# A hybrid decoder layer: the weight sums for the down projection move from VectorE to GpSimd, and the work around the end of the up projection is put in another order

## The reference

```python
h = h + rms_norm(mix @ w_out, attn_post_g)          # mix: two attention groups of 8 heads
u = rms_norm(h, mlp_pre_g)
a = jnp.square(jax.nn.relu(u @ w_up))               # w_up 1024 x 4096
h = h + rms_norm(a @ w_down, mlp_post_g)            # w_down 4096 x 1024
```

## Time and profile before

| | |
|---|---|
| device time, median of 3 runs | 611.48 us (611.33 to 612.48) |
| the profiled execution's own time | 612.76 us |
| its span, first to last instruction | 611.0 us |
| TensorE busy | 580.5 us (95%) |
| VectorE busy | 410.3 us (67%) |
| ScalarE busy | 310.6 us (51%) |
| GpSimd busy | 108.8 us (18%) |

### The profile page before, as it was taken

The page is one execution under the profiler, slowest core; times in us unless marked ns, Lnnn a source line. Parts: engine busy times, 40 slices in busy tenths (PEclk is TensorE's granted clock), DMA queues, the critical chain, the costliest instruction groups (busy, mean ns, idle before and its releaser), DMA issues.

```text
span 611.0 us, 8355 instructions
## 1 busy us (share of the span) xinstructions
PE 580.5 (95%) x2900; PEld 483.4 (79%) x2900; DVE 410.3 (67%) x787; ACT 310.6 (51%) x651; POOL 108.8 (18%) x165
## 2 busy tenths in 40 slices
PE   7999999999999999999999999999869999999995
PEld 7988898887787788997777777777748888888874
DVE  3448582788788408427657747757857897777797
ACT  5563262788898324544353352354324566555571
POOL 1153200346798101300000000000000000000034
PEclk9999999999999999999999999999998999999998
DMA  8441412000120082055877877777697555554503
GB/s 301 127 131 55 169 70 69 1 1 1 70 70 1 17 294 70 0 207 197 293 267 271 272 280 263 270 291 263 230 348 274 179 193 198 208 195 172 185 1 137
DMA packets 43777, 101.45 MB, mean 166 GB/s; under 512 B 3937, under 2 KB 22113, under 8 KB 39649
## 3 DMA queue, kind: packets, MB, share of 16 engines
q1 hardware_dynamic: 42704, 101.04, 46.9%
q10 hardware_dynamic: 1040, 0.00, 0.1%
HBM read 82.16 MB, written 18.87 MB: 165 GB/s over the span
## 4 chain that ended last, share of the span: by engine, by line
PE 59%; DVE 20%; ACT 10%; issue 5%; DMA 4%; DVEq 1%; SPq 0%; ACTq 0%; POOL 0%; POOLq 0%
PE bank L1188 19%; PE bank L1189 18%; PE bank L1190 18%; ACT w_hi L509 8%; DVE w_lo L797 6%; DVE stage L1083 5%; DVE relu L1062 3%; PE bank L1358 2%; DMA w_raw<-in_w_down 1%; DVE pT_lo L794 1%; ACT probs L621 1%; DVE bank L926 1%; DMA x_sb<-in_x 1%; DMA stage<-in_w_down 1%; DVE w_lo L794 1%
## 5 line engine op out<-in xcount | busy, mean ns | idle before, releaser
L1188 PE MATMUL bank<-uT_hi,w_hi 128*128 128x512 f32 (+1 forms) x280 | 105.5, 377 | 8.1 <-DVE w_lo L797 8.1
L1190 PE MATMUL bank<-uT_hi,w_lo 128*128 128x512 f32 (+1 forms) x280 | 103.9, 371 | 0.0
L1189 PE MATMUL bank<-uT_lo,w_hi 128*128 128x512 f32 (+1 forms) x280 | 103.9, 371 | 0.0
L509 ACT ACTIVATE w_hi<-w_raw 128x1024 fp32r<-128x1024 f32 (+2 forms) x65 | 62.7, 1010 | 72.4 <-PE bank L1190 63.8
L797 DVE SCALAR_TENSOR_TENSOR w_lo<-w_raw,g_up,w_hi 128x256 fp32r<-128x256 f32 x128 | 52.1, 481 | 66.9 <-ACT w_hi L509 66.9
L794 DVE TENSOR_TENSOR w_lo<-w_raw,w_hi 128x1024 fp32r<-128x1024 f32 (+1 forms) x57 | 67.8, 1232 | 40.8 <-ACT w_hi L509 40.6
L1188 PE MATMUL bank<-w_hi,a_hi 128*128 128x512 f32 x224 | 88.6, 396 | 6.9 <-DVE w_lo L794 6.9
L1189 PE MATMUL bank<-w_lo,a_hi 128*128 128x512 f32 x224 | 88.1, 393 | 0.0
L1190 PE MATMUL bank<-w_hi,a_lo 128*128 128x512 f32 x224 | 87.9, 392 | 0.0
L749 ACT ACTIVATE act_sb<-relu 128x512 f32 (+1 forms) x32 | 20.3, 635 | 106.1 <-DVE relu L1062 106.1
L1188 PEld LDWEIGHTS bank<-uT_hi,w_hi 128*128 128x128 f32 x280 | 52.7, 188 | 22.2 <-issue 13.5
(11 more groups left out here) (148 smaller groups left out, 1042.5 us busy)
## 6 DMA issues: line engine op xcount, KB each, us to landing
w_raw<-in_w_up SPq DMA_DIRECT2D x16, 1024.0 KB, 5.3
stage<-in_w_down SPq DMA_DIRECT2D x16, 1024.0 KB, 4.9
pair_sums<-stage SPq DMA_DIRECT2D x16, 1024.0 KB, 4.0
w_raw<-pair_sums SPq DMA_DIRECT2D x16, 1024.0 KB, 4.7
w_raw<-in_w_down SPq DMA_DIRECT2D x12, 1024.0 KB, 5.8
w_raw<-in_w_in SPq DMA_DIRECT2D x6, 1024.0 KB, 5.8
w_raw<-in_w_out SPq DMA_DIRECT2D x4, 1024.0 KB, 4.8
x_sb<-in_x SPq DMA_DIRECT2D x8, 256.0 KB, 6.0
```

The lines of the kernel that those rows point to most:

```text
L509: return nc.scalar.activation(out, whole, ACT.Copy, scale=scale)
L1188: nc.tensor.matmul(out, lh, rh, start=start, stop=False)
L1189: nc.tensor.matmul(out, lh, rl, start=False, stop=False)
L1190: return nc.tensor.matmul(out, ll, rh, start=False, stop=stop)
```

## The change

1. **Block sums on GpSimd.** `block_sums` leaves DVE. GpSimd does the same four differences for pairs 0 to 14, in straight-line code that waits for each load.
2. **The second bank's square.** ACT's square of bank m=1 of a half-step moves behind the high parts of the next chunk (`activation`).
3. **Activation parts of down chunk 0** (`down_a_hi(0)`, `down_a_lo(0)`), made after up step 0 before, are made with those of chunks 1 and 2 ahead of the last up step.
4. **Raw tile of chunk 2.** `raw_more[0]` moves to memory of its own behind `stage[1]`, and the chunk is loaded before chunk 1, with no wait for the end of up.
5. **Last pair.** Pair 15 is no longer staged. Its raw rows are loaded as chunk 23, the last of pass two, and DVE makes its four sums there, two in chunk 21 and two in chunk 22 (`last_block_sums`).
6. **Order near the end.** DVE's combines are spread: four before the low part of chunk 25, two after it, four after that of chunk 26. The squares of the first two row tiles' first halves move to chunk 12 on ACT, and GpSimd's scaling of them with it. The other squares and `scaled_y(2, 0)` come after the last chunk's parts.

```diff
-        raw_more = [sb(f"w_raw{i + 2}", [P, CW]) for i in range(2)]
+        raw_more = [None, sb("w_raw3", [P, CW])]
+        in_place_of_uT = sb("in_place_of_uT", [P, CW])
...
+        raw_more[0] = sb("w_raw2", [P, CW])
...  SP
-            for j in range(2):
-                down_chunk(j)
-                next_sums(NF // 4, j)
-            for j in range(2):
-                sp.wait_ge(stage_sums, 4 * (NF // 2 + j - 1))
-                store_sums(j, NF // 2 + j - 2)
+            down_chunk(0)
+            next_sums(NF // 4, 0)
+            down_chunk(2)
+            down_chunk(1)
+            for j in (1, 0):
+                sp.wait_ge(stage_sums, 4 * (NF // 2 - 1 - j))
+                store_sums(j, NF // 2 - 2 - j)
...  GpSimd
+            for n in range(NF // 2 - 1):
+                b11, b12, b21, b22 = (stage[n % 2][:, TOP * q:TOP * q + TOP] for q in range(4))
+                pool.wait_ge(stage_in[n % 2], 16 * (n // 2 + 1))
+                for m, (total, a, b) in enumerate(((b11, b12, b11), (b12, b22, b12), (b22, b22, b11), (b21, b21, b22))):
+                    if m:
+                        pool.wait_ge(stage_sums, 4 * n + m)
+                    nc.gpsimd.tensor_tensor(total, a, b, ALU.subtract).then_inc(stage_sums, 1)
...  ScalarE
+            def activation(i, tile):
+                act.wait_ge(relu_c, i * 4 + (tile + 1))
+                nc.scalar.activation(act_sb[:, bass.ds(i * 4 + tile, 1), :], relu[:, tile % 2:tile % 2 + 1, :],
+                                     ACT.Square).then_inc(a_ready, 1)
...
-                    for m in range(2):
-                        if last and j == 1 and m == 1:
-                            down_w_hi(1)
-                        act.wait_ge(relu_c, i * 4 + (2 * j + m + 1))
-                        nc.scalar.activation(act_sb[:, bass.ds(i * 4 + (2 * j + m), 1), :], relu[:, m:m + 1, :],
-                                             ACT.Square).then_inc(a_ready, 1)
+                        activation(i, 2 * j - 1)
+                    activation(i, 2 * j)
...
-            down_a_hi(0)
             with act.Fori(1, NF // 4 - 1) as i:
                 up_step(i)
-            down_a_hi(1)
-            down_a_hi(2)
+            for c in range(3):
+                down_a_hi(c)
             up_step(NF // 4 - 1, last=True)
+            down_w_hi(1)
+            activation(NF // 4 - 1, 3)
...
-                if c == NDOWN - 2:
+                if c == N1 + 4:
                     act.wait_ge(stage_out[0], 16 * (NF // 4))
-                    for t in (2, 3):
-                        for b in range(2):
-                            y_square(t, b)
+                    for t in range(2):
+                        y_square(t, 0)
...  VectorE
                             difference(i, j - 1)
-                            block_sums(i, j - 1)
-                            if last and j == 1:
-                                block_sums(i, j)
...
-                if c == NDOWN - 1:
-                    dve.wait_ge(g_post_in, 32)
-                    dve.wait_ge(comb, 10)
-                    scaled_y(2, 0)
                 down_w_lo(c)
                 if c == N1 + N2 + 1:
+                    finish(0)
+                if c == N1 + N2 + 2:
+                    finish(1)
                     for t in range(2):
                         dve.wait_ge(*((d_used, N1 + N2) if t else (p_full, 7)))
                         combine(ps[P4[t]][:, :], u3(t), ps[P4[t]][:, :])
+                if c in (N1 + N2 - 3, N1 + N2 - 2):
+                    last_block_sums(2 * (c - N1 - N2 + 3))
```

More of the change, by code:

```diff
@@ L380, in down_chunk @@
                     q = c - N1
-                    src, n = sums[q], 0
+                    src, n = (sums[q], 0) if q < N2 - 1 else (w_down_v[:, 2 * q:2 * q + 2, :], 2)
                 else:
@@ L1102, in _ @@
             up_step(0, first=True)
-            down_a_lo(0)
             with dve.Fori(1, NF // 4 - 1) as i:
                 up_step(i)
-            down_a_lo(1)
-            down_a_lo(2)
+            for c in range(3):
+                down_a_lo(c)
             up_step(NF // 4 - 1, last=True)
@@ L1111, in combine, with finish, last_block_sums @@
                 nc.vector.tensor_tensor(out, a, b, ALU.add).then_inc(comb, 1)
+            def finish(t):
+                dve.wait_ge(p_full, 5 + t)
+                dve.wait_ge(comb, 3 + t)
+                combine(ps[P7[t]][:, :], u3(t), ps[P5[t]][:, :])
+                combine(u2(t), u2(t), ps[P5[t]][:, :])
+            def last_block_sums(m0):
+                b11, b12, b21, b22 = (d_raw(N1 + N2 - 1)[:, TOP * q:TOP * q + TOP] for q in range(4))
+                sums = ((b11, b12, b11), (b12, b22, b12), (b22, b22, b11), (b21, b21, b22))
+                dve.wait_ge(*down_arrived(N1 + N2 - 1))
+                for m in (m0, m0 + 1):
+                    if m:
+                        dve.wait_ge(last_sums, m)
+                    nc.vector.tensor_tensor(*sums[m], ALU.subtract).then_inc(last_sums, 1)
             def scaled_y(t, n):
@@ L1169, in _ @@
                     token_sum((c - 7) // 2, 4)
+            dve.wait_ge(g_post_in, 32)
+            dve.wait_ge(comb, 10)
+            scaled_y(2, 0)
             un_halves = [un[:, 0:TOP], un[:, TOP:]]
```

40 lines of the change are left out of this document (16 added, 24 removed).

## The result

The changed kernel takes 606.05 us (median of 4 runs, 604.16 to 607.41), the kernel before on the same chip 611.98 (4 runs, 611.33 to 612.76): a ratio of 0.990, with a 95% interval from 0.987 to 0.9931. That is 5.9 us or 1% less, clear of no change but far from the 21.6 that were forecast; 589.9 was predicted and the range ended at 594.

A forecast was written before the change was run, and what follows sets the result against it. TensorE was taken to wait each half-step of up for a ring through ACT and DVE; 1.52 + 7.6 + 2.59 + 1.78 + 5.03 + 2.41 + 0.64 = 21.6 us off gave 589.9, range 588.7 to 594.

The forecast's parts named there:

- What bounds the kernel: From up on, TensorE loses 21.6 us to waits; in up a ring through ACT and DVE takes 11.57 against 10.88.
- The failed step, GpSimd: In up, GpSimd's four differences delay a half-step's eight low parts once, at most 1.3 us, leaving them 2.8 early.
- rival B: In up, GpSimd gets in between each two low parts: half-steps of 12.0, 15 us of gain lost, 605; chance 0.03.
- The second failed step, DMA: In up, DMA share rises from 0.78 to 0.83; a pair's load, sums and store fit its two half-steps, 21.8 us.
- Block sums off DVE: In up, with the square moved too, gains 7.6 us in half-steps 3 to 13; sums out alone shortens 11.57 to 8.8.
- Square behind: In up, the square's move shares the 7.6 us gain; moving chunk 0's activation parts gains 1.52 at half-step 2.
- Raw tile of chunk 2: At the start of down, the earlier load removes 5.03 us of waiting and 2.41 at the low clock.
- Order near the end: At chunk 25, spreading DVE's combines removes a TensorE wait of 0.64 us; the tail keeps its length.
- Back edge of TensorE's loop: In up's loop, seven passes of the back edge could cost 0 to 4.0 us; taken as 0, ACT's value.
- Rival A: Part of the handovers stays: back edge up to 0.57, early disturbed low parts, chunk 3 late; 591 to 594, chance 0.20.
- Rival C: In up, GpSimd's sums become the pace, slower overall from 3.1 us per operation; up to 650 us, chance 0.04.
- D: At the start of down, the clock stays low or chunk 2's load isn't what TensorE awaits: 600, chance 0.05.

The follow-up runs named there:

- store_first_phase: The changed kernel with the store issued ahead of the next up load on SyncE, and GpSimd's sums held until VectorE's low parts are through: 590.26 us.
- store_first: The changed kernel with the store of a pair's sums issued on SyncE ahead of the next up chunk's load, not behind it: 596.86 us.
- no_sums: The changed kernel with each of GpSimd's four differences of a pair replaced by a write of one column, all waits and transfers kept: 597.94 us.
- phase: The changed kernel with one more wait on GpSimd: pair n is summed only after VectorE's low parts of up chunk n+2: 600.63 us.
- sums_dve: The changed kernel with part 1 alone undone, so VectorE makes the block sums of pairs 0 to 14 again: 596.39 us.
- squares_only: The kernel before with parts 2 and 3 alone, sums still on VectorE: 611.06 us, ratio 0.9988.
- squares_store_first: The kernel before with parts 2 and 3, and the store issued ahead of the up load on SyncE: 597.90 us.
- old_squares: The changed kernel with part 2 alone undone, the second bank's square again ahead of the next high parts: 609.94 us.
- late_chunk2: store_first_phase with part 4 undone, so chunk 2's raw tile is loaded after the end of up: 592.39 us.

## Why the prediction was wrong

The direction was right, and so were the terms of down. The 13.5 us of up, the larger part of the sum, did not come: two rings that the prediction had ruled out or not counted took the old one's place. 5.9 us came of 21.6. By the prediction's own steps:

- **What bounds the kernel**: right. The ledger of TensorE's losses was 21.6; store_first_phase, which has all of the change's parts and no loss left in up and down, gained 611.0 - 588.4 = 22.6 of span and 21.8 us in the median. The 590.26 lies near the forecast of 589.9, but it is another kernel, with two orders added.
- **The failed step, GpSimd**: "GpSimd does not get in between DVE instructions that stand back to back. [...] So the eight low parts of a half-step wait once, for at most 1.3 us". It does get in. The low parts waited several times, 3.7 us in a half-step (3.25 to 6.98), and 4.4 in the first. The 2.66 us row, on which the step stood, shows one small instruction of GpSimd, on a tile of 128x1, that was held through VectorE's back-to-back work. Four differences of 128x512 are not held so, even when VectorE began first: in store_first they began 1.0 us into a burst of low parts, the first took 1.42 us, not much over the 1.285 of the earlier trace rows, and four of the low parts left were stretched all the same. Why the small instruction was kept out and these were not is open. This is rival B, which had a chance of 0.03; its price of 605 us is 1 from what was measured. That is in part luck: the loss is spread differently, with half-steps of 11.6, not 12.0, and 4.8 us in the first five, and the second ring, which B did not have, is as long. That low parts of 0.41 us alternate with GpSimd is shown by their starts and lengths; that the collision is the cause of their length, by no_sums, phase and sums_dve. That an exclusive lock passes from one to the other in between is the reading of the Trainium skill's "SBUF — State Buffer", Who interferes with whom, which says that the order of issue decides who blocks; no run here looks into the lock. It says nothing of instructions that stand back to back, though the prediction has it agree with its whole reading.
- **The second failed step, DMA**: "Store and up load are now issued together, and the slowest of `stage`'s transfers took 10.0 us [...] A pair has two half-steps, 21.8". The price was at hand, and was laid against the wrong budget. In the kernel before, this slowest transfer is a load into `stage`, the last of three 1 MB loads issued within 1 us (at 261.09, 261.50 and 262.01). In the changed kernel the store is the last of such a three. A pair has two half-steps for its data, but SyncE goes through its waits in order: load, up load, store, and the wait for the store's landing, once in each half-step. 0.9 + 0.7 + 10.0 = 11.6 is over 10.88. This ring was no rival, and holds the kernel at 596 to 601 where the collision is absent.
- **Block sums off DVE (part 1)**: undone, the kernel is 9.7 us faster (sums_dve, 9.0 by the ratios); with the store first it makes no difference (590.26 and 590.41). "Either half of the edit alone would shorten the ring" was right for the square: with it out, up's loop has no gap with the sums on VectorE. For the sums alone no run without the collision shows it.
- **Square behind (part 2), part 3**: right in kind. squares_only, which has just these two, takes out all waits of up's loop.
- **Raw tile of chunk 2 (part 4)**: the wait and the low clock went in the changed kernel, as forecast. The term of 5.03 + 2.41 = 7.4 was mis-sized as this part's own worth: undone, it costs 2.1. The rest goes with the earlier issue of the load, 0.20 us behind the end of up and not 5.35, and the shorter wait leaves the clock up. Most of this looks like the work of part 5, which the prediction put at nothing and which takes the last pair's sums and store out of SyncE's way. In squares_store_first, where up runs as smoothly but pair 15 is still staged, the load goes out 3.5 us behind the end of up, TensorE waits 4.42 us, not 1.79, and the clock falls. The two also differ in parts 1 and 6, and no run undoes part 5 alone, so its share is not shown. Chunk 3 came in time: no gap at any chunk of down.
- **Last pair in pass two (part 5)**: no cost in pass two, as forecast (what it may gain stands above); no gap in the 624 matmuls from half-step 15 to the end of pass two. A distance of 0.38 between two starts, 0.15 more than the pace, stands at the beginning of the third pass in every run but old_squares, where it is 0.66.
- **Order near the end (part 6)**: 0.64 forecast, 1.0 measured; the restart behind a wait of 0.68 costs more than the wait, 1.06 us from start to start. The tail kept its length (7.5 us from the last matmul's start to the end, 7.7 before).
- **Back edge of TensorE's loop**: 0 taken out of 0 to 4.0, and 0 it is: in sums_dve and squares_only the 672 matmuls of the loop's seven passes start at most 0.227 us apart. (The first up step, outside the loop, is not all in matmuls of 512 columns: 144 of its matmuls have 256.) Rival A had its 0.20 mainly from this, and did not occur; of its three causes only the disturbed low parts came, and not in the first steps alone. Rival C did not either: no operation of GpSimd came near 3.1 us in the mean (1.37). Nor did D: the clock and chunk 2 went as forecast.

Which of the two rings held the changed kernel? Both: ending the collision alone gives 596 to 601, shortening SyncE's ring by the store's place 596.86, and the two together 590.26. They are also coupled, since the landing of the pair's load starts GpSimd's sums (it waits 93.4 us for `stage` in the page), and when that lands depends on the store. So the single prices don't add up: 9.7 and 9.2 by the runs of sums_dve and store_first, 15.8 for both. Open is why the changed kernel scatters over 3.3 us (604.16 to 607.41) when store_first_phase stays within 0.13. The three slower executions had a mean granted clock of 0.990 to 0.991, the traced one 0.996, so they spent more time at the lower level. Where GpSimd's start falls against eight low parts could do that, by longer waits, but only one execution was traced.

## What to carry to other kernels

Count every engine's ring of waits in a stage as a rival pace, the DMA-issuing queue's too: from its first issue to its next, with the landing of whatever it waits for, as it will be when the issues stand close together; and issue first the transfer that the queue itself waits for. Work moved to GpSimd is not free for VectorE when GpSimd reads SBUF and VectorE's instructions have two inputs there: give it a fixed place behind the bursts on the critical path, or leave it on VectorE if that has room. A wait that vanishes in a loop can be asked back as one at its exit, so look at the exit before you believe in a gain, and before you discard an edit that "does nothing".

## What the runs showed of the hardware

- Four GpSimd differences that began 0.47 us before a burst of eight VectorE low parts (both kinds read two SBUF inputs) took 5.58 us, and the burst 6.98 where it takes 3.25 alone. Over all 60 differences of the changed kernel the mean is 1371 ns, against the 1285 of the earlier trace rows (7%). Differences that began 1.0 us into a burst (store_first) stretched it to 7.39. GpSimd memsets of 956 ns left it at 3.25 to 3.26.
- The same 1 MB store landed after 4.0 us when it was issued 3.7 us behind the up load, after 9.9 as the last of three issued within 1.6 us, and after 4.9 as the first of two. The up load, 5.2 to 5.4 us before, took 8.1 in the burst of three and 7.0 right behind the store (store_first_phase). In the kernel before, the last of three 1 MB loads issued within 1 us landed after 10.0.
- TensorE's loop has no visible back edge: the 672 matmuls of its seven passes start at most 0.227 us apart (sums_dve, squares_only).
- TensorE's clock after a wait: behind 1.79 us (late_chunk2), 2.73 (store_first) and 2.94 (old_squares, half-step 15) the matmuls started 0.23 apart; behind 2.82 (the changed kernel), 3.11 (sums_dve) and, from the fourth on, 4.42 (squares_store_first) they started 0.43 apart, the lower of the two levels. The length of the wait alone doesn't order the middle ones.
